# Input projections of an attention layer as two by two blocks with seven products

## The reference

```python
def token_mixers(x, cos, sin, w_in, lam_params, subln_g, w_bd, w_bs, w_o, lam_init):
    h = x @ w_in                      # (256 x 1024) @ (1024 x 5704)
    dq, dkk, dv, sq, sk, sv, iq, ik, iw, ga, gb = jnp.split(h, points, axis=-1)
    dq = partial_rope(...); dkk = partial_rope(...)
    ...
    ya = diff_attention(dq, dkk, dv, lam)                    # 4 heads
    ya = rms_norm_2(ya, subln_g) * (1.0 - lam_init)
    ...
    yb = dsa_attention(sq, sk, sv, iq, ik, iw, topk)         # 64 best keys by iq, ik, iw
    merged = jax.nn.sigmoid(ga) * (ya @ w_bd) + jax.nn.sigmoid(gb) * (yb @ w_bs)
    return merged @ w_o
```

## Time and profile before

| | us |
|---|---|
| median of 3 runs | 2425.26 |
| lowest and highest run | 2423.19, 2428.99 |
| the profiled execution, its own time | 2422.5 |
| its span in the trace | 2420.8 |

### The profile page before, as it was taken

One profiled execution on the slowest core, in us unless ns is written; L12 is line 12 of the kernel. 1 busy time (PEld: TensorE's weight loads), 2 busy tenths in 40 slices (PEclk: granted clock), 3 DMA queues, 4 the chain that ended last, 5 costly groups with the idle time before them and its releaser, 6 DMA issues. The chain is left out here.

```text
span 2420.8 us, 38035 instructions
## 1 busy us (share of the span) xinstructions
PE 2212.5 (91%) x16241; PEld 1313.2 (54%) x16241; DVE 876.8 (36%) x1736; ACT 404.7 (17%) x729; POOL 22.1 (1%) x114
## 2 busy tenths in 40 slices
PE   5978998889988999998998899989998899899996
PEld 3748888564438668666443455445443455444442
DVE  5877886632114111324221262133111352132112
ACT  1023332010001000321000123121001224021001
POOL 0000000000000000000000000000000000000000
PEclk8989998799999999999999999999999899999998
DMA  9900000899996665126999633466999433567996
GB/s 377 357 1 3 3 3 23 334 365 420 420 418 238 220 225 192 70 80 277 421 421 419 209 122 122 184 256 266 422 421 412 140 124 120 195 275 301 421 421 250
DMA packets 139912, 602.05 MB, mean 249 GB/s; under 512 B 34840, under 2 KB 37976, under 8 KB 84960
## 3 DMA queue, kind: packets, MB, share of 16 engines
q1 hardware_dynamic: 126912, 591.66, 62.2%
q10 hardware_dynamic: 12576, 7.89, 1.2%
q0 software_dynamic: 256, 0.02, 0.0%
HBM read 598.46 MB, written 1.05 MB: 248 GB/s over the span
## 5 line engine op out<-in xcount | busy, mean ns | idle before, releaser
L2366 PE MATMUL ps<-store 128*32 128x512 f32 (+1 forms) x2816 | 322.9, 612 | 32.7 <-DMA store<-in_moe_w_up 17.4
L3125 PE MATMUL ps<-store,x_features 128*128 128x512 f32 x704 | 321.3, 600 | 4.8 <-PEq L2948 2.5
L416 PE MATMUL ps<-store 128*128 128x512 f32 x480 | 215.1, 609 | 10.9 <-PEq L767 7.9
L2366 PEld LDWEIGHTS ps<-store 128*32 128x32 f32 x2816 | 89.9, 112 | 235.1 <-issue 231.9
L3125 PEld LDWEIGHTS ps<-store,x_features 128*128 128x128 f32 x704 | 127.7, 191 | 136.6 <-issue 134.4
L2324 PEld LDWEIGHTS ps<-store 128*128 128x128 f32 x1408 | 162.9, 192 | 35.1 <-issue 24.7
L2324 PE MATMUL ps<-store 128*128 128x128 f32 x1408 | 165.7, 275 | 8.9 <-DVE store L2501 7.1
L448 PE MATMUL ps<-x_features,store 128*128 128x256 f32 x768 | 166.8, 379 | 0.9 <-PEq L767 0.9
L2384 PE MATMUL ps<-store 128*32 128x512 f32 (+1 forms) x1408 | 159.5, 593 | 4.2 <-issue 2.3
L416 PEld LDWEIGHTS ps<-store 128*128 128x128 f32 x480 | 93.1, 196 | 128.6 <-issue 128.5
L2396 PE MATMUL ps<-store 128*128 128x512 f32 x352 | 159.1, 594 | 0.0
(11 more groups left out here) (431 smaller groups left out, 2319.7 us busy)
## 6 DMA issues: line engine op xcount, KB each, us to landing
store<-in_moe_w_gate SPq DMA_DIRECT2D x64, 1024.0 KB, 17.0
store<-in_moe_w_up SPq DMA_DIRECT2D x64, 1024.0 KB, 18.7
store<-in_moe_w_down SPq DMA_DIRECT2D x64, 1024.0 KB, 21.6
store<-in_w_exp_gate SPq DMA_DIRECT2D x64, 1024.0 KB, 14.9
store<-in_w_exp_up SPq DMA_DIRECT2D x64, 1024.0 KB, 16.9
store<-in_w_exp_down SPq DMA_DIRECT2D x64, 1024.0 KB, 18.2
store<-in_ada_w SPq DMA_DIRECT2D x48, 1024.0 KB, 13.9
store<-in_w_in SPq DMA_DIRECT2D x40, 1024.0 KB, 5.0
```

The source lines that it names most:

```text
L416: mm = pe.matmul(k.ps[:, set_ * 4 + tile * 2 + h, 0:n], xT[:, s, tile * P:(tile + 1) * P], w[:, kk, c0:c0 + n], start=(s == 0), stop=(s == ...
L2366: mm = pe.matmul(v3(k.ps[w * CAP:(w + 1) * CAP, 6, :], 2, F), xe[:, q % 2, s, w], both[:, :, s * F:(s + 1) * F], start=(s == 0), stop=(s = ...
L3125: mm = pe.matmul(k.ps[:, 2 * (j % 2) + tile, :], x, row[:, 0:HALF], start=(s_ == 0), stop=(s_ == K8 - 1))
```

## The change

Two neighbouring groups of 512 columns are now a pair. Its weights are four blocks (upper and lower half of the features, first and second group), its activations too (upper and lower half, first and second tile). Instead of eight block products of four 128-feature steps each, the pair takes seven, after a well-known scheme: some are made from sums of blocks. VectorE forms the sums of the activations once per stage (`s1` to `s4`, 128x512) and the sums of the weights in every pair (`across`, `between`, `below`, `rest`, 128x2048 each), and joins the seven products to the four results (`join`, 128x512 with one operand in PSUM). Some products are accumulated in PSUM on top of an earlier one.

TensorE's list has 4 + 7 x 5 = 39 steps; from step 4 each is one block product (`product`). The order in a pair is P1, P6, P7, P5, P2, P4, P3, into banks 0, 1, 2, 3, 0, 2, 3. The attention steps keep their instructions and get other numbers: the first unit starts at step 15 instead of quarter 16, the last at 34 instead of 37. VectorE's selection for the first tile is split over steps 9, 10, 12 and 13, for the second over 13 to 18. ScalarE copies one product and one result of each pair out of PSUM, and for the gates applies the sigmoid in SBUF to the three results that VectorE has joined. The weight units of a pair are loaded in another order, and two of its four slots are freed with its last product.

The core of the diff:

```diff
+QUARTETS, PRODUCTS = len(W_IN_HALVES) // 2, 7
+    def in_quartets(units):
+        return [units[4 * g + m] for g in range(QUARTETS) for m in (0, 2, 3, 1)]
...
-    JOBS = 1 + len(W_IN_HALVES)
-    QUARTERS = 4 * JOBS
-    TURN_INDEX, TURN_FIRST, TURN_SECOND = 6, 14, 27
+    STEPS = 4 + PRODUCTS * QUARTETS
+    TURN_INDEX, TURN_FIRST, TURN_SECOND = 6, 13, 26
     INDEX = (8, 10)
-    START = (16, 18, 20, 22, 28, 31, 34, 37)
-    TURN_YA, TURN_YB = 32, 42
+    START = (15, 17, 19, 21, 27, 30, 32, 34)
+    TURN_YA, TURN_YB = 31, 38
+    P1, P6, P7, P5, P2, P4, P3 = range(PRODUCTS)
+    RELEASES, OTHERS = {P6: 0, P7: 1, P3: 3}, (P1, P5, P2, P4)
+    U2, U3, C22, C21, C12 = range(1, 6)
...
+    s1, s2, s3, s4 = b.s1, b.s2, *(v3(s.take(4 * P), 4, P) for _ in range(2))
+    a11, a21, a12, a22 = (k.xT[:, 4 * h:4 * h + 4, tile * P:(tile + 1) * P] for h in range(2) for tile in range(TILES))
...
+    def wait_product(eng, g, p):
+        if p in RELEASES:
+            used_up(k, eng, block_unit(g, RELEASES[p]) + 1)
+        else:
+            eng.wait_ge(k.products_made.sem, k.products_made.at(len(OTHERS) * g + OTHERS.index(p) + 1))
+    def joined(g, n):
+        return k.blocks_joined.at(5 * g + n)
...
+            def product(g, p):
+                if p == P1:
+                    pe.wait_ge(k.columns_moved.sem, k.columns_moved.at(g + 1))
+                    landed(k, pe, block_unit(g, 0))
+                    x, w, at = a11, block_(g, 0), 0
+                elif p == P6:
+                    pe.wait_ge(k.blocks_made.sem, k.blocks_made.at(3 * g + 1))
+                    x, w, at = s2, b.between, 1
+                elif p == P7:
+                    pe.wait_ge(k.blocks_made.sem, k.blocks_made.at(3 * g + 2))
+                    if g:
+                        pe.wait_ge(k.blocks_joined.sem, joined(g - 1, C21))
+                    x, w, at = s3, block_(g, 1), 2
+                elif p == P5:
+                    if g:
+                        pe.wait_ge(k.blocks_joined.sem, joined(g - 1, C12))
+                    x, w, at = s1, b.across, 3
+                elif p == P2:
+                    landed(k, pe, block_unit(g, 3))
+                    pe.wait_ge(k.blocks_joined.sem, joined(g, U2))
+                    x, w, at = a12, block_(g, 3), 0
+                elif p == P4:
+                    pe.wait_ge(k.blocks_made.sem, k.blocks_made.at(3 * g + 3))
+                    pe.wait_ge(k.blocks_joined.sem, joined(g, U3))
+                    x, w, at = a22, b.between, 2
+                else:
+                    landed(k, pe, block_unit(g, 2))
+                    pe.wait_ge(k.blocks_joined.sem, joined(g, C22))
+                    x, w, at = s4, block_(g, 2), 3
+                for kk in range(4):
+                    mm = pe.matmul(k.ps[:, at, :], x[:, kk], w[:, kk * HALF:(kk + 1) * HALF], start=(kk == 0 and p < P2),
+                                   stop=(kk == 3), skip_group_check=True)
+                if p in RELEASES:
+                    mm.then_inc(k.used, 2 if p == P3 else 1)
+                else:
+                    mm.then_inc(k.products_made.sem, 1)
...
             def unit_values(u):
                 if u == 0:
+                    pe.wait_ge(k.columns_moved.sem, k.columns_moved.at(3))
+                    pe.wait_ge(k.blocks_joined.sem, joined(1, C21))
+                if u == DH:
                     pe.wait_ge(k.columns_moved.sem, k.columns_moved.at(4))
-                if u == DH:
-                    pe.wait_ge(k.columns_moved.sem, k.columns_moved.at(7))
+                    pe.wait_ge(k.blocks_joined.sem, joined(2, C12))
...
+            def first_out(g):
+                wait_product(act, g, P2)
+                act.activation(result(g, 0, 0), k.ps[:, 0, :], ACT.Sigmoid if gated(g) else ACT.Copy).then_inc(k.columns_moved.sem, 1)
+            def copy_first(g):
+                wait_product(act, g, P1)
+                act.activation(result(g, 0, 1), k.ps[:, 0, :], ACT.Copy).then_inc(k.block_copied.sem, 1)
+            def sigmoids(g):
+                act.wait_ge(k.blocks_joined.sem, joined(g, C21))
+                for c in range(2):
+                    k.act_chain.mark(act.activation(result(g, 1, c), result(g, 1, c), ACT.Sigmoid))
+                act.wait_ge(k.blocks_joined.sem, joined(g, C12))
+                k.act_chain.link(act, act.activation(result(g, 0, 1), result(g, 0, 1), ACT.Sigmoid))
...
+            def block_op(out, x, y, op):
+                link(vec.tensor_tensor(out, x, y, op))
+            def across(g):
+                landed(k, vec, block_unit(g, 0))
+                landed(k, vec, block_unit(g, 1))
+                if g:
+                    wait_product(vec, g - 1, P5)
+                block_op(b.across, block_(g, 1), block_(g, 0), SUB)
+            def between(g):
+                landed(k, vec, block_unit(g, 2))
+                if g:
+                    wait_product(vec, g - 1, P4)
+                block_op(b.between, block_(g, 2), b.across, SUB)
+                vec.sem_inc(k.blocks_made.sem, 1)
+            def below(g):
+                block_op(block_(g, 1), block_(g, 2), block_(g, 1), SUB)
+                vec.sem_inc(k.blocks_made.sem, 1)
+            def rest(g):
+                landed(k, vec, block_unit(g, 3))
+                wait_product(vec, g, P6)
+                block_op(b.between, block_(g, 3), b.between, SUB)
+                vec.sem_inc(k.blocks_made.sem, 1)
+            def join(g, out, x, at, p):
+                wait_product(vec, g, p)
+                block_op(out, x, k.ps[:, at, :], ADD)
+                vec.sem_inc(k.blocks_joined.sem, 1)
+            def blocks(g, p):
+                if p == P1 and g:
+                    join(g - 1, result(g - 1, 0, 1), result(g - 1, 0, 1), 3, P3)
+                if g == QUARTETS:
+                    return
+                if p == P1 and g:
+                    below(g)
+                if p == P6 + 1:
+                    vec.wait_ge(k.block_copied.sem, k.block_copied.at(g + 1))
+                    join(g, result(g, 0, 1), result(g, 0, 1), 1, P6)
+                    rest(g)
+                if p == P7 + 1:
+                    join(g, result(g, 1, 1), result(g, 0, 1), 2, P7)
+                if p == P5 + 1:
+                    join(g, result(g, 1, 1), result(g, 1, 1), 3, P5)
+                if p == P2 + 1 and g + 1 < QUARTETS:
+                    across(g + 1)
+                if p == P4 + 1:
+                    join(g, result(g, 1, 0), result(g, 0, 1), 2, P4)
+                    if g + 1 < QUARTETS:
+                        between(g + 1)
...
+            block_op(s1, a21, a22, ADD)
+            block_op(s2, s1, a11, SUB)
+            block_op(s3, a11, a21, SUB)
+            block_op(s4, a12, s2, SUB)
+            across(0)
+            between(0)
+            below(0)
...
-            for q in range(4, QUARTERS):
+            for q in range(4, STEPS + 1):
+                blocks(*divmod(q - 4, PRODUCTS))
...
                 if q == INDEX[0] + 1:
-                    select(0)
-                if q == 12:
-                    vec.wait_ge(k.columns_moved.sem, k.columns_moved.at(3))
+                    weigh(0)
+                if q in (10, 12):
+                    best_of(0, TOPK // 16)
+                if q == 11:
+                    vec.wait_ge(k.columns_moved.sem, k.columns_moved.at(2))
                     rotate(SEG["dq"], 16)
                     vec.sem_inc(k.rotated.sem, 1)
-                    select(1)
-                if q == 24:
-                    vec.wait_ge(k.columns_moved.sem, k.columns_moved.at(6))
+                if q == 13:
+                    hide_rest(0)
+                    weigh(1)
+                if q in (14, 15, 16, 17):
+                    best_of(1, TOPK // 32)
+                if q == 18:
+                    hide_rest(1)
+                if q == 25:
+                    vec.wait_ge(k.columns_moved.sem, k.columns_moved.at(4))
                     rotate(SEG["sq"], 16)
                     vec.sem_inc(k.rotated.sem, 1)
```

More of the change, by code:

```diff
@@ L3049, in second_buffers @@
     b.lam = c.take(4)
+    b.across, b.between = c.take(SLOT), c.take(SLOT)
+    b.s1, b.s2 = (v3(c.take(4 * P), 4, P) for _ in range(2))
+    b.lp = v3(c.take(4 * HN), 4, HN)
     b.end = c.at
@@ L3198, in unit_values @@
                 mm.then_inc(k.units_valued.sem, 1)
-            for q in range(QUARTERS):
+            for q in range(STEPS):
                 if q == TURN_INDEX:
@@ L3227, in _ @@
                         unit_scores(u)
-                quarter(q)
+                if q < 4:
+                    quarter(q)
+                else:
+                    product(*divmod(q - 4, PRODUCTS))
         @block.scalar
```

92 lines of the change are left out of this document (51 added, 41 removed).

## The result

The changed kernel takes 2439.98 us (median of 6 runs, 2434.16 to 2444.65) where the kernel before takes 2426.32 in runs beside it: a ratio of 1.0059, interval 1.0039 to 1.0079. It is slower by 13.7 us. The forecast was 2431.0, so slower was right and the size was not: 5.7 us were foreseen, under half of what came.

A forecast was written before the change was run, and what follows sets the result against it. TensorE was taken to bound the stage; per layer 17.3 us of removed products against added waits gave +2.7, plus 0.3 for the clock, so 2425.3 became 2431 us. Range 2420 to 2440.

The forecast's parts named there:

- the first block product: Front of the layer: TensorE waits 1.5 us for bank 0, which ScalarE is still emptying of the index columns.
- the first unit's transposes: Step 17: TensorE's list takes 28.8 us, VectorE's up to mixing the probabilities 37.5; TensorE waits 8.7 us.
- the third unit's: Third attention unit's transposes: VectorE waits for TensorE twice and mixes until 10.65 against 8.9; TensorE waits 1.8 us.
- the second attention's: Transposes of the second attention's queries, step 26: VectorE's join, block sum and rotation take 5.8 against 3.46; wait 2.3 us.
- the second unit's: Second attention unit's transposes: VectorE's list takes 14.2 us against TensorE's 8.9; TensorE waits 5.3 us.
- The step that failed: Clock loss behind the 8.7 us pause, at most 3.4 us, disappears in the next wait; 0.3 us a layer charged.
- The sum without the clock: Per layer, 17.3 us of removed products against the added waits and a longer end: +2.7 us.
- the rival called Clock: The second pause of a layer costs the clock too, unhidden: 3.4 us more a layer, 2438 us; chance 0.15.
- quicker than summed: Rival: VectorE's block sums take less than the row's time, so the kernel is faster, 2414 at half; chance 0.12.
- The case with nothing to measure: Rival: signals free or some small pieces overlapping, between -4 and +3 us, 2421 to 2428; chance 0.21.
- free signals: Lower bound if VectorE's signals cost nothing: waits 7.8, 4.8, 1.6 and 2.1, a layer +0.7 or +0.8, 2427 us.
- What would have shown it: Signs: 3.46 us steps, 280 block products, waits of 8 to 9, 4 to 5.5, about 2, about 2, VectorE gapless some 50 us.

The follow-up runs named there:

- the kernel with fillers: Changed kernel plus 17 products a layer that nobody reads, right before four places where TensorE waits for VectorE; 2433.46 us, 1.0041 to the kernel before.
- the kernel with pauses: Kernel before, with TensorE waiting for two GpSimd stores at three quarters a layer; 2440.91 us, 1.0073 to the kernel before.
- the seven edited kernels with seven products: Changed kernel with fillers, short block sums, later selection, signals sent by instructions, other banks, or three repairs without and with fillers; 2405.54 to 2438.81 us.
- the two kernels with pauses or products: Kernel before with three TensorE pauses a layer, 2440.91 us, or with two unread products at each of those places, 2433.55 us.

## Why the prediction was right in its waits and wrong in its size

**The removed products, the block sums, the joins and the signals** came as priced: 2292 and 688 ns, and 0.11 to 0.18 for a signal (behind a block sum 0.15 to the next instruction, behind a join 0.21, without one 0.03 to 0.04) where 0.12 was charged.

**The waits** came as added up. At the first block product 1.34, or 1.5 with what it delays (forecast 1.5), at the first unit's transposes 8.69 and 8.84 (8.7), at the third unit's 1.73 (1.8), at the second attention's 2.22 and 2.21 (2.3), at the end 0.38 more (0.4). At the second unit's it was 3.18 in the first profile and 2.56 in the second, where 5.3 stood in the sum: the loss of the clock behind the first wait, 1.8 and 2.4 (from the transposes to the next product 7.36 and 7.97, 5.54 in the kernel with fillers), had gone before, and adds to 5.0 with either. The forecast said that the first loss would disappear there, and it did.

**The step that failed** is the clock: "Its loss, at most half of 6.8, 3.4 us, falls on work that ends in the next wait of 5.3 and disappears there; the second pause shrinks by it. Hence 0.3, with 0 and 3.4 as ends." It stopped at the first pause. The shrunk one at the second unit (2.6 to 3.3 us) and the one at the second attention (2.2) brought the clock down in all four stages of the two profiles, the one at the third unit (1.7) in one of the four, for 3.4 us each (6.8 behind the longest), and no later wait takes this up: the third one comes behind the second, but stays at 1.73, since VectorE itself waits there for products of TensorE. The work behind such a pause tells the price: from the second unit's transposes to the product after the values 7.12 us, 5.53 in the kernel with fillers, 1.6 lost; 1.66 behind the next, 1.68 at the second attention's (7.01 against 5.33).

The sum without the clock came out near what was measured. The kernel with fillers shows 3.0 a layer (1.5 and 1.5), the forecast had 2.7. This is luck in part: the waits were summed about 0.6 too long, a short wait that both lists have shrank from 0.92 to 0.48, and the overlap of neighbouring products that each pause takes away, some 0.25 by the kernel with pauses, stood in no term. The clock term is the difference between the block part with fillers and the four of the changed kernel: 4.9, 3.5, 3.3 and 5.0 (taking 171.8), 4.2 as a mean, where the forecast had 0.3. With 3.9 more a layer the forecast of +5.7 becomes +13.5, against +13.7 measured.

That it closes so well on the medians is luck too. By theirs, the seven edited kernels with seven products lie 2 to 7 us higher over the kernel before than their block parts and the 1.5 add up to, the two kernels with pauses or products 1 to 2; only the changed kernel lies 0.7 lower. What this is stays open. A part may be the end of the stage: its pause grew from 1.53 to 1.91, and behind it, in the next stage, the clock fell in three of the four cases of the two profiles of the changed kernel, never in the four of the kernel before.

So the rival called Clock described what happened, at 3.4 a layer and 2438, and 0.15 was too low a chance for it. What I held against it, that the second pause is only 2 to 4 us long, was no argument: no row of this stage in the kernel before has a pause of that length, harmless or not. Other stages of it have them. There are six pauses of 1.77 to 3.31 us with TensorE at work at 1.00 for 5 us ahead of them and at work for 5 us behind them, and the granted clock fell behind three (2.26, 3.29 and 3.31) and not behind the others (1.77, 2.21 and 2.37). Two of the six by stretches, ahead of and behind the pauses of 2.26 and 2.37:

```profile
1311.85:1316.85 5.00, 4.99 (x24) 1.89 (x12) 1.39 (x3) 0.00 (x0) 0.00 (x0) 1.00 1.01 418
1319.11:1324.11 5.00, 5.00 (x32) 1.46 (x36) 0.00 (x0) 0.00 (x0) 0.00 (x0) 0.66 1.01 419
...
2374.66:2379.66 5.00, 5.00 (x24) 1.89 (x12) 1.38 (x3) 0.00 (x0) 0.00 (x0) 1.00 1.01 421
2382.03:2387.03 5.00, 5.00 (x48) 1.65 (x52) 0.00 (x0) 0.00 (x0) 0.00 (x0) 1.00 1.01 421
```

The prediction used only the long pause of the earlier trace rows; these six would have spoken for counting a fall behind about half of the short ones. The Trainium skill, "TensorE: Matmul & The Clock Gate", section HAM oscillation, says of a kernel that waits for loads between its bursts of products that every such wait costs the array its full rate again. By that rule the term had to be counted once for each pause; the traces agree for nine of the twelve short pauses of the changed kernel, and for about half of those in all kernels (last section).

**The other rivals.** VectorE was not quicker than summed. The case with nothing to measure needed free signals, and a signal that is an instruction has its price; sent by the instruction that it stands for, it has none. On this the Trainium skill, "VectorE: DVE Perf Modes", section The DRAIN you can't avoid, says that a semaphore after each instruction costs nothing extra. The trace agrees for one that the instruction sends itself, with a gap of 0.03 us, and not for a signal that is an instruction, with 0.15 to 0.21.

**Readings of the prediction that do not hold.** The second layer's stage does not repeat the first within 0.1 us in the kernel before: it takes 189.25, since the granted clock is low at its start, and only the block parts repeat.

```profile
1886.12:2075.37 189.25, 186.80 (x646) 96.91 (x647) 66.32 (x174) 52.84 (x119) 1.28 (x3) 0.99 0.40 130
```

With free signals the first wait comes to 7.5 by the forecast's own figures (ten by 0.12 off 8.7), not 7.8; without signal instructions it measured 7.63. The waits as listed there make +0.9 a layer, not +0.7 or +0.8. And half of 2.292 us is 1.15, not 1.26. None of this moves the forecast.

**What would have shown it** was named rightly: the waits, VectorE's stretch without a gap, the step of 3.43 to 3.46 us. The granted clock behind each pause was not on that list.

## What to carry to other kernels

Count a pause of the busiest engine twice: its length, and the work behind it at the lower clock, unless another wait swallows it. Here the loss behind the first pause of a row was hidden in the next wait, and the losses behind the last ones were not. Work that is moved to an engine with room in the mean must also find room at its place in the list: here the same sums cost 13.7 us beside the selection of keys and came to 12.1 less than the kernel before once the selection stood elsewhere, two units started a step earlier, the signals were sent by the instructions and the index columns had other banks. Before an exact comparison, cut the trace where chance comes in: the block part repeated within 0.01 us in the kernel before, whole runs within some 14.

## What the runs showed of the hardware

I had expected short pauses to leave the clock alone. In the profiles of all these kernels the block parts have 40 pauses of TensorE of 1.7 to 3.4 us (the long first one of some kernels not counted), and behind 21 of them the granted clock fell to 0.50, for 3.4 us each time but one (6.8 us, behind the longest pause, 3.34); behind those of 1.5 us and less it never did. Length alone does not decide: two of 2.85 us left it up, and behind those of 1.73 and 1.74 it fell three times in six. The Trainium skill, "TensorE: Matmul & The Clock Gate", section What's actually happening, says that the same kernel meets the change of the clock at another point in each run. The two profiles of the changed kernel agree: behind the 1.73 of the first layer the clock fell in one of them. What decides in a single case stays open here.
